# A hybrid diffusion step on one core: layer-norm totals by one-column matmuls, and the mean spread by ones times partial sums

## The reference, cut to what matters

```python
def layer_norm(x, g, b):
    xf = x.astype(jnp.float32)
    mu = xf.mean(-1, keepdims=True)
    var = jnp.square(xf - mu).mean(-1, keepdims=True)
    return ((xf - mu) * lax.rsqrt(var + LN_EPS) * g + b).astype(x.dtype)
...
for layer in range(DEPTH):                      # DEPTH = 4
    ...                                         # op, os_ = mixer(modulate(...))
    yp = layer_norm(ALPHA * yp + mp[2] * op, ln_g[layer, 0], ln_b[layer, 0])
    ys = layer_norm(ALPHA * ys + ms[2] * os_, ln_g[layer, 0], ln_b[layer, 0])
    fp = swiglu(modulate(yp, mp[3], mp[4]), ffn_wg[layer], ffn_wu[layer], ffn_wd[layer])
    fs = swiglu(modulate(ys, ms[3], ms[4]), ffn_wg[layer], ffn_wu[layer], ffn_wd[layer])
    yp = layer_norm(ALPHA * yp + mp[5] * fp, ln_g[layer, 1], ln_b[layer, 1])
    ys = layer_norm(ALPHA * ys + ms[5] * fs, ln_g[layer, 1], ln_b[layer, 1])
```

## Time and profile before

| | |
|---|---|
| median of 3 runs | 3717.49 us (3706.36 to 3722.47) |
| profiled execution, its own time | 3714.42 us |
| its span, first to last instruction | 3712.6 us |
| PE busy | 3410.7 us (92%) |
| DVE busy | 2282.0 us (61%) |
| ACT busy | 927.6 us (25%) |
| GpSimd (POOL) busy | 1911.4 us (51%) |
| mean granted TensorE clock | 0.969 |

### The profile page before, as it was taken

One profiled execution on the slowest core, in us unless ns is written; L12 is line 12 of the kernel. 1 busy time (PEld: TensorE's weight loads), 2 busy tenths in 40 slices (PEclk: granted clock), 3 DMA queues, 4 the chain that ended last, 5 costly groups with the idle time before them and its releaser, 6 DMA issues.

```text
span 3712.6 us, 72727 instructions
## 1 busy us (share of the span) xinstructions
PE 3410.7 (92%) x30948; PEld 3213.7 (87%) x30948; DVE 2282.0 (61%) x3263; ACT 927.6 (25%) x1893; POOL 1911.4 (51%) x1510
## 2 busy tenths in 40 slices
PE   7888999999789788889999994999999999999998
PEld 6666899999789678888999993899998777999997
DVE  4667778787872667646774869774766555611115
ACT  4323230001353345542300013300013333310010
POOL 4686446565355556525565651465654223455552
PEclk9999999999899889999999997999999999999999
DMA  5211134443245443322343430343432000222221
GB/s 200 74 63 52 54 123 160 144 142 112 77 171 177 128 103 93 84 84 90 120 136 120 144 99 32 115 152 120 131 110 75 14 18 26 67 74 74 74 74 52
DMA packets 227434, 367.57 MB, mean 99 GB/s; under 512 B 105328, under 2 KB 111664, under 8 KB 226992
## 3 DMA queue, kind: packets, MB, share of 16 engines
q1 hardware_dynamic: 169872, 250.82, 22.6%
q10 hardware_dynamic: 57248, 112.18, 8.8%
HBM read 326.41 MB, written 36.54 MB: 98 GB/s over the span
## 4 chain that ended last, share of the span: by engine, by line
PE 78%; DVE 13%; ACT 3%; issue 2%; DMA 1%; SPq 1%; ACTq 0%; POOL 0%; DVEq 0%; POOLq 0%
PE ps L934 60%; PE ps L1198 3%; PE ps L984 2%; PE ps L1229 2%; PE ps L1211 2%; PE ps L1170 1%; DVE x L2453 1%; DVE x L2462 1%; PE ps L1152 1%; DVE m_mx L2592 1%; DVE late_acc L2611 1%; DVE ps L2844 1%; DVE m_PT L2601 1%; DVE s_T L2843 1%; PE ps L1329 1%
## 5 line engine op out<-in xcount | busy, mean ns | idle before, releaser
L731 POOL TENSOR_SCALAR w_hi<-w_raw 128x1024 fp32r<-128x1024 f32 x354 | 401.3, 1134 | 1210.4 <-PE ps L934 922.1
L934 PE MATMUL ps<-f_hlo,w_hi 128*128 128x320 f32 x2688 | 612.7, 309 | 0.0
L934 PE MATMUL ps<-f_hhi,w_lo 128*128 128x320 f32 x2688 | 612.4, 309 | 0.0
L934 PE MATMUL ps<-f_hhi,w_hi 128*128 128x320 f32 x2688 | 612.2, 309 | 0.0
L2350 DVE SCALAR_TENSOR_TENSOR f_acc<-f_unit,silu_c,f_acc 128x512 f32<-128x512 f32 x532 | 601.0, 1170 | 8.2
L736 POOL TENSOR_TENSOR w_lo<-w_raw,w_hi 128x512 fp32r<-128x512 f32 x354 | 555.9, 1570 | 0.0
L734 POOL TENSOR_TENSOR w_lo<-w_raw,w_hi 128x512 fp32r<-128x512 f32 x354 | 501.6, 1417 | 29.5
L934 PEld LDWEIGHTS ps<-f_hhi,w_hi 128*128 128x128 f32 x2688 | 449.6, 188 | 0.0
L934 PEld LDWEIGHTS ps<-f_hlo,w_hi 128*128 128x128 f32 x2688 | 449.3, 188 | 0.0
L934 PEld LDWEIGHTS ps<-f_hhi,w_lo 128*128 128x128 f32 x2688 | 449.1, 188 | 0.0
L1757 ACT ACTIVATE f_sil<-ps 128x640 f32<-128x640 f32 x88 | 62.1, 705 | 1264.9 <-PE ps L934 1264.8
(11 more groups left out here) (410 smaller groups left out, 6550.8 us busy)
## 6 DMA issues: line engine op xcount, KB each, us to landing
w_raw<-in_w SPq DMA_DIRECT2D x340, 512.0 KB, 3.6
f_unit<-in_ada_w ACTq DMA_DIRECT2D x76, 1024.0 KB, 5.9
up_scratch<-r_o ACTq DMA_DIRECT2D x40, 320.0 KB, 2.5
late_step<-in_ada_w SPq DMA_DIRECT2D x48, 256.0 KB, 3.5
ada_ring<-in_ada_w SPq DMA_DIRECT2D x8, 1024.0 KB, 6.8
s_LW<-up_scratch SPq DMA_DIRECT2D x16, 320.0 KB, 4.9
s_LA<-up_scratch SPq DMA_DIRECT2D x8, 640.0 KB, 7.2
x<-in_x SPq DMA_DIRECT2D x1, 2560.0 KB, 13.3
```

The source lines that it names most:

```text
L731: nc.gpsimd.tensor_scalar(whi[:, slot, :], raw[:, raw_slot, :], 1.0, 0.0, ALU.mult, ALU.add).then_inc(w_hi_done, 1)
L934: last = mm(ps[:, 2 * b + h, 0:HT], w, r[:, h * HT:(h + 1) * HT], start=kt == 0 and n < 2, stop=kt == KT - 1 and n >= 4)
```

## The change

`turned` goes. In its place `columns` multiplies each piece of 128 tokens, as the stationary operand, by one column of ones, so that the sum over the 128 partitions arrives as one column of PSUM per piece; partial sum and last block are accumulated there. `everywhere` multiplies ones by the partial sum and later by the last block, and leaves the total, not yet divided, on all partitions. DVE's four reductions and the diagonal of the mean go, the division moves into `centred`, and the six idle matmuls after the totals go; those after `spread` stay.

```diff
-q_ln = uses("ln", dict(... acc=2, tr=4, rd=1, var=1, sd=1, diag=2, bc=2, cen=KD, nrm=KD), 2 * DEPTH)
+q_ln = uses("ln", dict(... acc=2, tr=2, var=1, sd=1, diag=1, bc=2, cen=KD, nrm=KD), 2 * DEPTH)
...
-            def turned(t, src, b):
-                out = ps[:, 2 * b:2 * b + 2, :].rearrange("p b c -> p (b c)")
-                for j in range(NCH):
-                    last = nc.tensor.transpose(out[:, j * P:(j + 1) * P], src[:, j * P:(j + 1) * P], ident)
-                last.then_inc(q_ln[t].tr, 1)
+            def columns(src, b, first=False):
+                for j in range(NCH):
+                    last = mm(ps[:, b, j:j + 1], src[:, j * P:(j + 1) * P], ones[:, 0:1], start=first and j == 0, stop=not first,
+                              skip_group_check=True)
+                return last
+            def everywhere(src, first=False):
+                for h in range(2):
+                    last = mm(ps[:, 6 + h, 0:HT], ones, src[:, h * HT:(h + 1) * HT], start=first, stop=not first)
+                return last
...
                 pe.wait_ge(q.acc, q.at.acc + 1)
-                turned(t, m.S[:, 0, :], 2)
+                columns(m.S[:, 0, :], 4, True)
+                everywhere(m.S[:, 0, :], True)
+                pe.wait_ge(upd, at + KD)
+                columns(x[:, KD - 1, :], 4).then_inc(q.tr, 1)
                 pe.wait_ge(q.acc, q.at.acc + 2)
-                turned(t, m.S[:, 1, :], 3)
-                pe.wait_ge(upd, at + KD)
-                turned(t, x[:, KD - 1, :], 0)
+                columns(m.S[:, 1, :], 5, True)
                 pe.wait_ge(q.sq, q.at.sq + KD)
-                turned(t, m.S[:, 3, :], 1)
-                pe.wait_ge(q.rd, q.at.rd + 1)
-                run_on(2)
+                columns(m.S[:, 3, :], 5).then_inc(q.tr, 1)
+                everywhere(x[:, KD - 1, :]).then_inc(q.bc, 1)
...
-                for n in range(2):
-                    pe.wait_ge(q.diag, q.at.diag + n + 1)
-                    for h in range(2):
-                        last = mm(ps[:, 6 - 2 * n + h, 0:HT], ones, m.diag[n][:, h * HT:(h + 1) * HT], start=True, stop=True)
-                    last.then_inc(q.bc, 1)
+                pe.wait_ge(q.diag, q.at.diag + 1)
+                for h in range(2):
+                    last = mm(ps[:, 4 + h, 0:HT], ones, m.diag[1][:, h * HT:(h + 1) * HT], start=True, stop=True)
+                last.then_inc(q.bc, 1)
...
-                total(1, 2).then_inc(q.rd, 1)
-                dve.wait_ge(q.rd, q.at.rd + 1)
-                ch(total(2, 3))
...
-                stt(cols[:, 5, :], cols[:, 4, :], 1.0 / D, cols[:, 2, :], ALU.mult, ALU.add).then_inc(q.var, 1)
-                diagonal(0, 0)
+                dve.wait_ge(q.tr, q.at.tr + 1)
+                ch(ts(cols[:, 1, :], ps[:, 4, 0:NCH], -1.0 / D, None, ALU.mult))
+                ch(tt(cols[:, 2, :], cols[:, 1, :], cols[:, 1, :], ALU.mult))
+                dve.wait_ge(q.tr, q.at.tr + 2)
+                stt(cols[:, 5, :], ps[:, 5, 0:NCH], 1.0 / D, cols[:, 2, :], ALU.mult, ALU.subtract).then_inc(q.var, 1)
...
-                    tt(halves(x[:, k, :]), halves(x[:, k, :]), pair(3), ALU.add).then_inc(q.cen, 1)
+                    xs = halves(x[:, k, :])
+                    stt(xs, pair(3), -1.0 / D, xs, ALU.mult, ALU.add).then_inc(q.cen, 1)
```

More of the change, by code:

```diff
@@ L484, in build @@
         q_split = dict(zip(splits, uses("split", dict(val=KD, hi=KD, lo=KD), len(splits))))
-        q_ln = uses("ln", dict(ksum=1, d=2, sh=KD - 2, sq=KD, cp=2, red=4, acc=2, tr=4, rd=1, var=1, sd=1, diag=2, bc=2, cen=KD, nrm=KD), 2 * DEPTH)
+        q_ln = uses("ln", dict(ksum=1, d=2, sh=KD - 2, sq=KD, cp=2, red=4, acc=2, tr=2, var=1, sd=1, diag=1, bc=2, cen=KD, nrm=KD), 2 * DEPTH)
         ln_fin = sem("ln_fin")
@@ L2421, in scales @@
                 m, q = m_ln[t], q_ln[t]
[L2423 to L2426, removed]
                 def diagonal(n, c):
```

## The result

The changed kernel takes 3725.36 us (median of 20 runs, 3715.8 to 3733.44), the kernel before 3714.02 us in 20 runs beside it. The ratio is 1.0032, with a 95% interval of 1.0025 to 1.0039. The profiled execution is the longest of the twenty, 3733.44 us with a span of 3731.7, so its lengths need not be typical; it is read for where within a norm the clock changes. Its mean granted clock is 0.961; before it was 0.969. With two levels, 1.00 and 0.50, that makes (1 - 0.961)/0.5 x 3731.7 = 291 us at half clock, against (1 - 0.969)/0.5 x 3712.6 = 230 before. The granted clock of the eight stretches from the last update to the first multiplication says where: 46 us of half clock lie in the norms themselves, against 2 before.

What follows compares the result with a forecast made beforehand. The prediction took the kernel as bound by its projections on PE, with DVE setting the end in the norms; +2.1 us for seven norms and +3 for the fifth, together +5 on 3714.4, gave 3719.5, put at 3720, range 3704 to 3731.

Steps and rivals of the forecast that it cites:

- The queue and its prices: PE's six groups per norm: four `columns` sets at 1.11 us, two `everywhere` calls at 1.08; variance no earlier.
- The gain of 0.82 a norm: Behind the variance, at full clock, the first multiplication starts at 3694.35 instead of 3695.17, 0.82 us earlier.
- The clock: In the norms, narrow matmuls replacing transposes let PE's clock fall and eat the gain: 3720, range 3712 to 3731, chance 0.5.
- Rival 2: The clock holds through the norms, kept by the `everywhere` calls and the rest: 3708.9, chance 0.37.
- Rival 3: Clock falls ahead of the first sets in most norms, still half at `twins`: +4.6 us each, 3751, chance 0.06.
- Rivals 4 and 5: Columns cheaper than the two-column row: 3690, chance 0.03; or next stages wait for something else: 3714 to 3718, chance 0.04.
- +0.3 for each of seven norms: Net loss in us per norm except the fifth from the clock's fall, part given back behind it; 2.1 us together.
- some +0.9: Middle of the loss in us per norm over cases with one set and spread, spread alone, or two sets slow.
- may only move: The half-clock stretch already in the first `twins` behind a norm may only shift, giving back part of the loss.
- +3: Loss in us in the fifth norm, where PE starts slow with three more sets before wide work; bounds +0.2 and +5.3.
- upper bound of +5.3: Fifth norm's loss in us with four sets, two calls and the spread all at half clock, 2.2 each.
- cases 1, 2 and 5: Clock falls (3720, chance 0.5), clock holds (3708.9, 0.37), next stages wait for something else (3714 to 3718, 0.04).

Runs made afterwards that it cites:

- e3: Kernel before with totals by one-column matmuls, the mean still by a diagonal, six unread matmuls kept behind the columns: 3753.21 us, ratio 1.0122.
- e1: Changed kernel with its 20 one-column matmuls per norm streaming 96 columns of ones instead of one: 3714.33 us, 1.0001 to the kernel before.
- e2: Kernel before with transposes and reductions kept, but the mean by `everywhere`; first diagonal and six unread matmuls behind the totals gone: 3717.16 us, 1.002.
- e4: Kernel before without the six unread matmuls behind the totals, nothing else changed: 3731.79 us, 1.006.
- g8: e1 plus eight unread matmuls ahead of the fifth norm, behind its sixth block update: 3707.27 us, 1.0001 to the kernel before.
- h2: e1 plus g5's unread matmuls and, in the fifth norm, eight unread ones behind block 6 and three behind block 7: 3703.93 us, 0.9986.
- g5: e1 plus small unread matmuls in PE's waits in the first panel behind a norm: 3707.98 us, 1.0002 to the kernel before.
- h1: e1 repeated unchanged on another chip: 3708.51 us, 0.9999 to the kernel before.
- g6: Kernel before plus the same small unread matmuls in the first panel behind a norm as g5: 3705.15 us, 0.9996.

## Why the prediction was right, and where its sizes were off

**The queue and its prices: right.** A set at 1.11 us, a call at 1.08 (measured 1.09 to 1.11), the set behind the last block 0.78 us late (0.78), the variance no earlier (4.30 against 4.33), the first `centred` 0.86 us earlier (0.87), one wide `centred` at 0.82 (two take 1.55, as two of TENSOR_TENSOR do in e3). The gain of 0.82 a norm at the full clock is what e1 shows: its seven norms without the fifth sum to 55.71 against 61.71, 0.86 each.

**The clock: the mechanism right.** It falls in seven norms of the changed kernel, with PE busy all the time ahead of the fall, and the fifth stays at 0.50 from its start. e1 changes nothing but the streamed columns, and the clock stays up in seven norms, and the 0.3% is gone. Rival 2, that the clock holds, falls. It had leaned on the Trainium skill's "TensorE: Matmul & The Clock Gate", whose Part 1 (HAM oscillation) ties a fall of the clock to idle gaps of PE. Such gaps do stand ahead of a fall in the traces: 2.75 us in e2, though only in some of its norms, 3.70 in e4 and 3.63 in g8. What the prediction drew from it, that the clock holds where there is hardly a gap, is refuted by the last norm of the changed kernel, which loses it without any. Part 4 (PE-mode transpose) of the same page of the Trainium skill says that the full clock does not engage for transposes; like the earlier trace rows, e4's fifth norm speaks against it, with a rise behind 3.40 us of nothing but transposes. Rival 3 needed three slow sets in most norms, and only the fifth has them. Rivals 4 and 5 fall too: a set costs 1.11, and the shifts of the norms do reach the stages here, though in the wide kernels the gain hardly reaches the time.

**Mis-sized: "+0.3 for each of seven norms".** They measured +1.00, -0.17, +0.86, -0.01, +0.29, +1.67 and +0.33, sum 3.97 or +0.57 each. The prediction's cases were the right ones. Where only `spread` is slow (norms 6 and 8) it is the +0.3 worked out for that (norm 4 is like them, but had a variance 0.3 us later before); with a set or two as well (1, 3, 7) it is +0.86 to +1.67, against +1.0 to +1.4. The +0.3 was the middle of the cases, "some +0.9", less a discount, because the slow stretch of `twins` "may only move". The norms alone came out between the two, as four of the seven lose 0.33 us at most. The discount was the mistake: the stages gave nothing back, and those behind norms 1, 3 and 5 are longer after than before (477.58, 477.99 and 477.95 us against 476.37, 476.90 and 475.34), while those behind 6 and 7 changed by -0.50 and -0.02, some +4.4 us together between these two profiles.

**Mis-sized: "+3" for the fifth norm.** It measured +5.60, just over the upper bound of +5.3 that the prediction worked out with every group at half clock. The bound's own terms, four sets, two calls and the spread at 2.2 each, make 15.4 us, and PE took 15.34 from its start at 2332.16 to the first multiplication at 2347.50, against 9.74 before; the right difference is 5.7, so that the bound was added up 0.4 short. The bound was the case itself: PE started at half clock, and the clock did not rise before `spread`. The part of the sum for the full clock was off as well. With 96 columns this norm takes 9.87 us, +1.24 where 1.0 lost and 0.8 won back had made +0.2. The prediction let the clock rise at the same moment as before, 1.77 us behind the update; in e1 it rose 3.19 behind it. The slow start that follows PE's 14 us of idle time was left over in the wide kernels, and only h2's unread matmuls remove it (7.79).

**The time.** The prediction put 5.1 us on top of the profiled execution; the medians differ by 11.3. Of the difference between the two profiles the norms are 9.57, so the sizes above are the miss in the main. Some of the closeness is luck: the sum of 3719.5 was rounded up to 3720 beside a median of three runs of 3717.5, and the twenty runs have 3714.0, so that the forecast stands 6.0 above the kernel before and only 5.4 under the measured time. And the range of 3704 to 3731 holds cases 1, 2 and 5 alike, so the time alone does not tell them apart; the traces and e1 do. `run_on` behind `spread` was to take twice 3.40 us in some norms; it takes 4.29 at most (norm 3), since the clock rises in the midst of it.

**What stays open.** In e1, g5, g8 and h1 the norms are 4.8 to 5.1 us shorter than before, 0.13%, and the times are 1.0001, 1.0002, 1.0001 and 0.9999, where 0.9987 would be whole. Each interval alone reaches to within 0.0005 of that or past it, but four together speak for a gain that is given back. The clock gives a lead. Over all runs its mean is 0.9682 in e1 and 0.9683 in h1, against 0.9692 and 0.9696 for the kernel before beside them. That is 7 to 10 us more at half clock, nearly all of it outside the norms, which hold 3 us of half clock in e1's profile. Work at half clock takes twice as long, so by this estimate 4 to 5 us at most are lost there. No run tests it. g5 against g6 shows where not: the stages behind norms 1, 3, 5, 6 and 7 agree within 0.03 us. The stage behind norm 4 (pooling) takes 80.92 us in g5 and 80.01 in g6, which would be 0.9 of the 1.07 won there, yet in h1 it takes 79.97. The stage behind norm 2 (RWKV) varies from 782.5 to 792.5 us among the profiles, more than the effect, and what lies ahead of the first norm, where no kernel was changed, from 458.6 to 468.9. One profile for each kernel cannot settle it.

## What to carry to other kernels

Price a matmul that replaces another by what it does to the clock for the work behind it, and not by its own duration: a one-column float32 matmul keeps PE's records full and did not keep the clock. Where a matmul takes as long with 96 columns as with one, as here, stream the 96, if PSUM has the room. The clock that this kept is shown for these norms alone; 32 columns kept it in two of eight. Before removing work that nobody reads, look at what the granted clock is behind it.

## What the runs showed of the hardware

- Ten float32 matmuls of 128x128 by 1 or by 96 columns take the same time on PE at the full clock, 2.23 and 2.24 us; at half clock a set of five one-column ones took 1.99 (2336.59 to 2338.58) to 2.15 (2332.16 to 2334.31), 1.8 to 1.9 times half of that, and four records of 128x320 took 2.28 (2334.31 to 2336.59) against 1.11, twice.
- With PE busy for every microsecond of 2335.35 to 2342.10 in one-column matmuls and one call of `everywhere`, the clock stayed at 0.50.
- In g8 the clock stood at 1.00 while PE idled for 3.63 us, and fell to 0.50 within 0.3 us of the start of its next work.
- In e4's fifth norm the clock rose from 0.50 to 1.00 behind 3.40 us in which PE ran nothing but float32 transposes of 128x128.
